# Keys and values of a recurrence turned by VectorE and 1 KB row moves instead of TensorE, in a hybrid decoder block on one core

## The reference, cut to what matters

```python
kb = k * beta[..., None]
vb = v * beta[..., None]
lower = jnp.where(strict, jnp.einsum('bhncd,bhnsd->bhncs', kb, k) * decay, 0.0)
a_mat = lower + jnp.eye(c)
# u, w = a_mat^-1 [vb, kb * exp(gc)]
def step(state, inp):
    v_new = u_n - w_n @ state
    o = (q_n * exp(gc_n)) @ state + qk_n @ v_new
    k_dec = k_n * jnp.exp(g_last - gc_n)
    state = state * exp(g_last) + k_dec^T @ v_new
```

## Time and profile before

| | |
|---|---|
| median of 3 runs | 1113.17 us (1113.09 to 1113.29) |
| profiled execution, own time | 1113.16 us |
| its span in the trace | 1111.3 us |
| PE busy | 1100.7 us, 99% |
| DVE busy | 537.6 us, 48% |
| ACT busy | 447.2 us, 40% |
| POOL busy | 539.2 us, 49% |
| TensorE clock granted | 0.999 of full (2.4 GHz) |

### The profile page before, as it was taken

The page is one execution under the profiler, slowest core; times in us unless marked ns, Lnnn a source line. Parts: engine busy times, 40 slices in busy tenths (PEclk is TensorE's granted clock), DMA queues, the critical chain, the costliest instruction groups (busy, mean ns, idle before and its releaser), DMA issues.

```text
span 1111.3 us, 15998 instructions
## 1 busy us (share of the span) xinstructions
PE 1100.7 (99%) x5679; PEld 924.1 (83%) x5679; DVE 537.6 (48%) x1202; ACT 447.2 (40%) x731; POOL 539.2 (49%) x338
## 2 busy tenths in 40 slices
PE   9999999999999999999999999999999999999997
PEld 8788888889898888888888888888888888888886
DVE  5666547476767567777777563241221222220003
ACT  6475453333332455555555324323232222221124
POOL 5445774343432456555555445804444444444444
PEclk9999999999999999999999999999999999999999
DMA  7233344332423454443443474502333333322231
GB/s 215 78 106 103 95 114 119 92 105 85 106 74 98 123 134 117 129 132 114 118 115 107 145 233 146 176 1 80 103 100 96 94 94 94 94 94 98 98 108 76
DMA packets 173602, 122.55 MB, mean 110 GB/s; under 512 B 6769, under 2 KB 160474, under 8 KB 173554
## 3 DMA queue, kind: packets, MB, share of 16 engines
q1 hardware_dynamic: 156208, 98.46, 30.7%
q10 hardware_dynamic: 17346, 23.44, 6.8%
HBM read 113.45 MB, written 8.44 MB: 110 GB/s over the span
## 4 chain that ended last, share of the span: by engine, by line
PE 96%; DVE 1%; issue 1%; ACT 1%; DMA 0%; POOL 0%; ACTq 0%; POOLq 0%; DVEq 0%
PE ps L1768 65%; PE ps L2188 10%; PE ps L1882 7%; PE ps L2108 4%; PE ps L1721 3%; PE ps L2062 2%; PE ps L2162 1%; PE ps L2033 1%; PE ps L2032 1%; PE ps L1818 1%; PE ps L1830 0%; ACT Zm L919 0%; DMA x_nat<-in_x 0%; PE ps L1841 0%; DVE ps L1385 0%
## 5 line engine op out<-in xcount | busy, mean ns | idle before, releaser
L583 POOL TENSOR_TENSOR w_lo<-raw,w_hi 128x1024 fp32r<-128x1024 f32 x159 | 383.2, 2410 | 498.3 <-ACT w_hi L772 485.9
L1768 PE MATMUL ps<-h_hi,w_lo 128*128 128x512 f32 x960 | 376.6, 392 | 0.0
L1768 PE MATMUL ps<-h_hi,w_hi 128*128 128x512 f32 x960 | 376.6, 392 | 0.0
L1768 PE MATMUL ps<-h_lo,w_hi 128*128 128x512 f32 x960 | 376.6, 392 | 0.0
L772 ACT ACTIVATE w_hi<-raw 128x1024 fp32r<-128x1024 f32 x159 | 168.6, 1060 | 492.9 <-PE ps L1768 391.2
L1768 PEld LDWEIGHTS ps<-h_hi,w_lo 128*128 128x128 f32 x960 | 180.4, 188 | 37.2 <-issue 0.4
L1768 PEld LDWEIGHTS ps<-h_hi,w_hi 128*128 128x128 f32 x960 | 180.4, 188 | 36.7 <-POOL w_lo L583 0.4
L1768 PEld LDWEIGHTS ps<-h_lo,w_hi 128*128 128x128 f32 x960 | 180.4, 188 | 36.3
L1661 DVE TENSOR_TENSOR f_lo<-tmp,f_hi 128x512 f32 (+1 forms) x22 | 41.7, 1895 | 143.6 <-ACT f_hi L1113 143.6
L1239 DVE SCALAR_TENSOR_TENSOR tmp<-ps,prm,tmp 128x511 f32<-128x511 f32 (+2 forms) x72 | 53.9, 749 | 46.9 <-ACT tmp L832 45.2
L1629 DVE TENSOR_TENSOR mixT<-ps,mixT 128x512 f32<-128x512 f32 x16 | 11.0, 689 | 125.2 <-PE ps L2188 108.2
(11 more groups left out here) (302 smaller groups left out, 1598.3 us busy)
## 6 DMA issues: line engine op xcount, KB each, us to landing
raw<-in_w_in SPq DMA_DIRECT2D x79, 512.0 KB, 3.9
raw<-in_w_gate SPq DMA_DIRECT2D x22, 512.0 KB, 3.8
raw<-in_w_up SPq DMA_DIRECT2D x22, 512.0 KB, 3.9
raw<-in_w_down SPq DMA_DIRECT2D x22, 512.0 KB, 3.3
gate_dram<-gate ACTq DMA_DIRECT2D x24, 256.0 KB, 2.0
cum<-cum_dram ACTq DMA_DIRECT2D x8, 512.0 KB, 7.1
raw<-in_w_branch_a SPq DMA_DIRECT2D x8, 512.0 KB, 3.8
raw<-in_w_branch_b SPq DMA_DIRECT2D x8, 512.0 KB, 3.7
```

What stands on the lines that cost most here:

```text
L583: pool.tensor_tensor(w_lo[:, r % 2, :], raw[:, r, :], w_hi[:, r % 2, :], ALU.subtract)\
L1768: return pe.matmul(ps[:, bank, :], wts[wl][k], acts[xl][:, k, :], start=(n == 0), stop=(n == len(PASSES) - 1))
```

## The change

DVE transposes keys and values itself, in blocks of 32x32, from `qkv` into `Tm` and `Yn`. Such a transpose leaves each block in the partitions where it was, so 16 transfers per tensor carry the blocks to the right 32 partitions: each takes 32 rows of 1 KB (one block of each of 8 heads) from one group of partitions to another, values into `Vb`, keys into `Eb`. ACT starts them (`kv_move`), 16 for the values and 16 for the keys (none for the keys in the last chunk). ACT scales in `kv_scale`: `Vb` in place and `Kd` from `Eb`, eight instructions each. PE no longer turns anything, and its waits for `o_ready` and `S_ready` stand later. The readers of `Vb` see each head as four pieces of 32 columns. `fill_done` is split into `fill_high` (high part of unit n+2) and `fill_take` (copy and transfer of unit n); for unit n+1 the take now stands behind the right half of `Zm`.

```diff
@@ -161,6 +161,9 @@
             cv = tmp
             X = Yn
             w = Tm
+            k_parts, Vb_parts, k_blocks, v_blocks = (
+                t[:, :, :].rearrange("p h c -> p (h c)").rearrange("p (b h j) -> p b h j", h=H, j=LINE)
+                for t in (Eb, Vb, Tm, Yn))
             sums = Lc[:, :, :].rearrange("p h s -> p (h s)").rearrange("p (t n) -> p t n", t=TT)
             smT = Kd[0:64, 0:4, :].rearrange("p a n -> p (a n)")
             sq = [o[:, 4 * a:4 * a + 4, :].rearrange("p h c -> p (h c)") for a in range(2)]
@@ -403,6 +406,14 @@
 
             return t.unsqueeze(2).broadcast_to([P, t.shape[1], C])
 
+        def parts(t):
+
+            return t.rearrange("p (b j) -> p b j", j=LINE)
+
+        def moved(c):
+
+            return 16 * (NB // 2) ** 2 * (2 * c + 2 if c < TT - 1 else 2 * c + 1)
+
         def half(t, q):
             return t[:, 4 * q:4 * q + 4, :]
 
@@ -668,7 +679,7 @@
                 pool.wait_ge(E_exp, 2 * c + 1)
                 pool.wait_ge(row_step, 2)
                 if c > 0:
-                    pool.wait_ge(L_ready, 2 * c)
+                    pool.wait_ge(Kd_ready, c * H)
                 pool.tensor_tensor(Eb[:, :, :], E[:, :, :], heads(bn2[:, c * H:c * H + H]), ALU.mult)\
                     .then_inc(Eb_ready, 1)
 
@@ -891,11 +902,14 @@
                     act.wait_ge(of_turned, led(of_turned, a + 1))
                     act.activation(mixT[:, 4 * a:4 * a + 4, T - C:T], bank4(a), ACT.Copy).then_inc(oT_ready, 1)
 
-            def fill_done(n):
+            def fill_high(n):
+
+                high_ahead(GATE0 + n // 4, n % 4)
+
+            def fill_take(n):
 
                 c, u = divmod(n, FILL)
                 q, r = GATE0 + n // 4, n % 4
-                high_ahead(q, r)
                 if n >= TT * FILL:
                     return
                 act.wait_ge(unit_done, 4 * q + r + 1)
@@ -907,17 +921,52 @@
                 act.wait_ge(fill_taken, led(fill_taken, n + 1))
                 act.dma_start(gate_dram[u // 2, c * 2 + u % 2], gate[:, n % 2, :]).then_inc(s, 16)
 
+            def fill_done(n):
+
+                fill_high(n)
+                fill_take(n)
+
+            def kv_move(c):
+
+                act.wait_ge(kv_blocks, 2 * c + 2 if c < TT - 1 else 2 * TT - 1)
+                if c > 0:
+                    act.wait_ge(S_done, 2 * c)
+                    act.wait_ge(w_done, led(w_done, 2 * c))
+                for dst, src in ((Vb_parts, v_blocks), (k_parts, k_blocks)):
+                    if dst is k_parts and c == TT - 1:
+                        continue
+                    if dst is k_parts:
+                        act.wait_ge(L_ready, 2 * c + 2)
+                    for b in range(NB // 2):
+                        for t in range(NB // 2):
+                            act.dma_start(dst[t * LINE:(t + 1) * LINE, b], src[b * LINE:(b + 1) * LINE, t])\
+                                .then_inc(kv_moved, 16)
+
+            def kv_scale(c):
+
+                act.wait_ge(kv_moved, moved(c))
+                act.wait_ge(row_step, 3)
+                for h in range(H):
+                    act.activation(Vb_parts[:, :, h, :], Vb_parts[:, :, h, :], ACT.Copy,
+                                   scale=bn[:, c * H + h:c * H + h + 1]).then_inc(Vb_ready, 1)
+                for h in range(H if c < TT - 1 else 0):
+                    act.activation(parts(Kd[:, h, :]), k_parts[:, :, h, :], ACT.Copy,
+                                   scale=gexp[:, 1, c * H + h:c * H + h + 1]).then_inc(Kd_ready, 1)
+
             def chunk(c):
                 n = c * FILL + AHEAD
                 fill_done(n - 1)
+                kv_move(c)
                 if c < TT - 1:
                     load_rows(c + 1)
                 fill_done(n)
-                fill_done(n + 1)
+                fill_high(n + 1)
                 act.wait_ge(W_done, c + 1)
                 for b in range(NB // 2, NB):
                     act.activation(Zm[:, :, b * BS:(b + 1) * BS], Wb[:, :, :], ACT.Copy,
                                    scale=own_neg[:, b:b + 1]).then_inc(Z_right, 1)
+                fill_take(n + 1)
+                kv_scale(c)
                 fill_done(n + 2)
                 if c < TT - 1:
                     decay(c + 1)
@@ -1350,15 +1399,14 @@
 
             def chunk(c):
                 rq = rn[:, c * 2 * H:c * 2 * H + H]
-                for a in range(2 if c < TT - 1 else 0):
-                    dve.wait_ge(k_turned, c * 2 + a + 1)
-                    dve.tensor_tensor(half(Kd, a), bank4(a),
-                                      heads(gexp[:, 1, c * H + 4 * a:c * H + 4 * a + 4]), ALU.mult)\
-                        .then_inc(Kd_ready, 1)
-                for a in range(2):
-                    dve.wait_ge(v_turned, c * 2 + a + 1)
-                    dve.tensor_tensor(half(Vb, a), bank4(4 + a), heads(bn[:, c * H + 4 * a:c * H + 4 * a + 4]), ALU.mult)\
-                        .then_inc(Vb_ready, 1)
+                if c > 0:
+                    dve.wait_ge(S_done, c * 2)
+                for dst, src in ((v_blocks, 2 * H), (k_blocks, H)):
+                    if dst is k_blocks and c == TT - 1:
+                        continue
+                    dve.transpose(dst.rearrange("p b h j -> p h b j"),
+                                  qkv[:, src:src + H, c * C:c * C + C].rearrange("p h (b j) -> p h b j", j=LINE))\
+                        .then_inc(kv_blocks, 1)
 
                 dve.wait_ge(E_cut, c * 4 + 4)
                 dve.wait_ge(G_done, c * 2 + 2)
@@ -1378,7 +1426,6 @@
                     dve.wait_ge(qk_done, c * 2 + a + 1)
                     dve.tensor_tensor(half(qkT, a), bank4(a), half(ET, a), ALU.mult).then_inc(qk_ready, 1)
                 dve.wait_ge(Lc_step, c * 2 + 2)
-                dve.wait_ge(Vb_ready, c * 2 + 2)
 
                 def spread(row):
 
@@ -1411,6 +1458,7 @@
 
                 dve.wait_ge(Z_left, c * (NB // 2) + NB // 2)
                 dve.wait_ge(Z_right, c * (NB // 2) + NB // 2)
+                dve.wait_ge(kv_moved, moved(c))
                 for a in range(2):
                     dve.transpose(half(Tm, a).rearrange("p h c -> p (h c)"), half(Zm, a).rearrange("p h c -> p (h c)"))\
                         .then_inc(T_ready, 1)
@@ -1445,13 +1493,13 @@
                     dve.wait_ge(of_ready, led(of_ready, c))
                     turn_outputs(c - 1, BLOCKS[:7])
 
-                dve.wait_ge(Vb_ready, c * 2 + 2)
+                dve.wait_ge(Vb_ready, c * H + H)
                 dve.wait_ge(row_step, 3)
                 dve.wait_ge(Zd_done, c * 6 + 6)
                 for h in range(H if c > 0 else 0):
                     dve.wait_ge(ks_done, c * 2 - 2 + h // 4 + 1)
-                    dve.scalar_tensor_tensor(out=X[:, h, :], in0=bank4(h // 4)[:, h % 4, :],
-                                             scalar=c1[:, c * H + h:c * H + h + 1], in1=Vb[:, h, :], op0=ALU.mult,
+                    dve.scalar_tensor_tensor(out=parts(X[:, h, :]), in0=parts(bank4(h // 4)[:, h % 4, :]),
+                                             scalar=c1[:, c * H + h:c * H + h + 1], in1=Vb_parts[:, :, h, :], op0=ALU.mult,
                                              op1=ALU.add).then_inc(X_ready, 1)
                 if c > 0:
                     turn_outputs(c - 1, BLOCKS[7:])
@@ -1913,17 +1961,10 @@
                         last = do(h, 4 * a + h)
                     last.then_inc(sem_, 1)
 
+                for a in range(2):
+                    per_head(a, lambda h, n: mm(bank4(2 + a)[:, h, :], kT(n), kT(n)), G_done)
                 if c > 0:
                     pe.wait_ge(o_ready, led(o_ready, c * 2))
-                for a in range(2 if c < TT - 1 else 0):
-                    per_head(a, lambda h, n: turn(bank4(a)[:, h, :], kT(n)), k_turned)
-                pe.wait_ge(S_ready, led(S_ready, c * 8))
-                for a in range(2):
-                    per_head(a, lambda h, n: turn(bank4(4 + a)[:, h, :], vT_(n)), v_turned)
-                for a in range(2):
-                    per_head(a, lambda h, n: mm(bank4(2 + a)[:, h, :], kT(n), kT(n)), G_done)
-                if c < TT - 1:
-                    pe.wait_ge(Kd_ready, c * 2 + 2)
                 for a in range(2):
                     per_head(a, lambda h, n: mm(bank4(a)[:, h, :], kT(n), qT(n)), qk_done)
                 fill(FILLS[0])
@@ -1972,6 +2013,7 @@
                 fill(FILLS[5])
 
                 if c > 0:
+                    pe.wait_ge(S_ready, led(S_ready, c * 8))
                     for a in range(2):
                         per_head(a, lambda h, n: mm(bank4(a)[:, h, :], kT(n), S[:, n, :]), ks_done)
                 pe.wait_ge(Z_ready, c * 2 + 2)
@@ -1983,9 +2025,9 @@
                     if c > 0:
                         pe.wait_ge(X_ready, led(X_ready, c * 8 - 8 + 4 * a + 4))
                     else:
-                        pe.wait_ge(Vb_ready, 2)
-                    rhs = X if c > 0 else Vb
```

(9 more changed lines are left out.)

## The result

The changed kernel takes 1150.85 us (median, 1150.42 to 1151.59), the one before 1113.23 in the same comparison (1113.09 to 1113.45). The ratio is 1.034 with a 95% interval of [1.033, 1.035]. The forecast was 1118.4 with a range up to 1127: the side was right, the size was not, and the time lies outside the range. The profiled execution took 1151.59 us.

The account below looks back on a forecast made before the run. PE, busy 1100.7 of 1111.3 us, was taken to bound the kernel: 1113.2 - 6.1 (turns) - 1.2 (waits for `Zm`) + 12.5 (stalls in three chunks) = 1118.4 us, with a range of 1106.3 to 1127.

Parts of the forecast that it names:

- The issue of the transfers: ACT starts 32 transfers per chunk at 0.38 us each, delaying unit n+2's high part; PE stalls 12.5 us over three chunks.
- 32 rows can be spread over as many engines: Reason given for taking 0.38 us per transfer on ACT, close to a 128-row transfer's 0.338 + 0.04.
- The formula around it: PE's stall per chunk, waiting for unit n+2's low part, is 32p - 8.1 us for a pitch of p per transfer.
- In the last chunk: no stall: With 16 transfers ACT is done at T+8.3, before PE finishes unit n at T+8.9, so PE does not wait.
- Removed from PE: 56 turns of keys and values leave PE at 0.109 us each, 6.1 us, all on the path.
- the moved gate copy: Unit n+1's copy and transfer behind the masks let ACT start `Zm` earlier; up to 0.3 us per chunk in a rival.
- Transposes on DVE at no cost: Two transposes of 128x1024, 1.3 us each, fit DVE's free 5.9 us before `Lq` at T+2.06; cost nothing.
- Scaling on ACT at no cost: 16 scaling instructions in three chunks, 4.3 us, fit the 6 us or more ACT has free behind `Zm`; cost nothing.
- One stall takes the place of all others: Work queued behind ACT's transfers, `Zm`, `ET` and DVE's wait for `kv_moved` included, is ready before the stalled PE needs it.
- The third rival: The moves drain slowly, so DVE's wait for `kv_moved` ends last, from 0.56 us per transfer; 1140 to 1145 us, chance 0.05.
- the stall for `w_lo`: PE waits at line 1816 for POOL's low part of unit n+2, three times, each 2.6 to 6 us.
- 32 p: Time ACT needs to issue a chunk's 32 transfers at pitch p; at 0.38 it is 12.2 us.

Follow-up runs that it names:

- PE kept busy: The changed kernel with 50 extra unused products on PE in each of the first three chunks, where PE stood; 1149.37 us, ratio 1.033.
- first DRAM version: The changed kernel with the blocks sent over DRAM, four stores and one load per tensor instead of 16 moves; 1111.55 us, ratio 0.998.
- SP version: The changed kernel with all 112 moves started by SP instead of ACT, ahead of its load of unit n+5; 1141.35 us, ratio 1.021.
- first kernel of the last experiment: The blocks over DRAM, `ET`'s transfer ahead of the loads, against which the loads moved behind the high part of unit n+3; 1107.75 us, ratio 0.995.

## Why the prediction was wrong

- *The issue of the transfers* is the step that failed, as a term of the sum that was sized too small. Its pitch was taken as 0.38 with an upper bound of 0.50, from transfers with an end in DRAM. It is 0.639. "32 rows can be spread over as many engines" was an argument from rows for a number that hardly depends on them. The formula around it was right: 32 x 0.639 - 8.1 = 12.3 us, and 12.65, 12.59 and 12.34 were measured.
- *"In the last chunk: no stall"* failed by the same number: 16 x 0.639 puts the end of the issues at T+12.4 instead of T+8.3, the low part at T+16.1, and PE comes at T+14.4. 1.50 us was measured.
- *The clock* was in no term and no bound. It cost 6.9 us, shown by the products of PE kept busy (3.31 us for 14, not 6.00). With both, 1113.2 - 7.6 + 39.1 + 6.9 is the measured time.
- *Removed from PE*: 6.1 us, right (6.8 without the stall, of which 0.8 is the moved gate copy, there put at up to 0.3 in a chunk).
- *Transposes on DVE at no cost*: right. Two of 1.25 and 1.20 us (1.3 predicted from the earlier trace rows), and `Lq` starts at 164.03, T+2.06; the timeline of DVE in the first chunk:

```profile
160.05 1.25 DVE L1407 STREAM_TRANSPOSE Yn<-qkv 128x1024 f32<-128x1024 f32 x1
161.22 1.20 DVE L1407 STREAM_TRANSPOSE Tm<-qkv 128x1024 f32<-128x1024 f32 x1
...
164.03 1.31 DVE L1414 TENSOR_TENSOR Lq<-ps,Lq 32x256 f32<-32x256 f32 x3 [1.61 <-PE ps L1930]
```

- *Scaling on ACT at no cost*: right, by the kernel with one transfer per tensor. The 16 instructions took 4.9 us, where 4.3 was put. *"One stall takes the place of all others"*: right; nobody waited for `kv_moved`, which by 1.9 us of landing comes before the late `Zm`.
- *The third rival* had its threshold at 0.56 per transfer, and the pitch passed it, but with ACT as the issuer the stall for `w_lo` comes first and is priced by the same 32 p. Its number, 1140 to 1145, was the nearest of all by luck, for a wait that did not occur (and its own price of 10 to 13 us in each of three chunks gives 1136 at the lower end). Nor did the moves go one after another at 0.95 us each: issued 0.64 apart, they landed 1.9 us later each. Had the forecast's formula been carried to 0.64, it would have given 1143, and 1145 with the stall of the last chunk. The bounds came from the nearest rows, and no row had both ends in SBUF.

## What to carry to other kernels

Count the transfers that an engine issues ahead of its computing, and price them by kind: in these runs 0.61 us each back to back within SBUF and 0.44 to 0.50 with an end in DRAM, nearly whatever they carry (single ones in a busy kernel took up to 1.7). If a permutation needs many within SBUF, fewer and larger ones over DRAM can be cheaper, with the loads put where they don't hold up a transfer that others wait for. When an operand lands late, look also at what its reader then runs beside. And price a stall of PE above its length: after one of 12 us the next products ran at half clock.

## What the runs showed of the hardware

- An issue on ACT takes the same time for 1 row as for 128, and for 32 rows of 1 KB as of 4 KB (608, 622; 515, 526 ns); 8 rows took 669. On SP it took 0.59 in the median, with 0.63 to 0.70 from one to the next.
- A short wait can cost more clock than a long one: behind 12.65 us of standing PE ran at 0.50 for some 6 us, behind 2.4 us (the first DRAM version) for 15, and in the SP version, behind 4.9 us, at a mean of 0.54 over 30 us in which it was busy for 27. What decides how long stays open; the runs don't show it.
- A VectorE product of 0.28 us took up to 1.99 when a GpSimd instruction ran beside it, and ended 0.08 us behind it; with 1 MB of loads in flight and GpSimd nearly through, four of them took 0.87 us together, as usual.
- The landing of `ET` (512 KB) went from 6.2 us to 8.0 and 8.3 (medians) with 1 MB of loads issued just ahead of it or behind it. It isn't the loads alone: in the first chunk of the first kernel of the last experiment they were issued 7.1 us after it, and it took 7.9.
